# Column sums for a normalizer, tile positions of small products and whole-tile transposes in a two-layer streaming encoder

## What is computed

```
# mLSTM, per head (8 heads of 512), block by block
s = einsum('bhtd,bhsd->bhts', q, k) * d                      # pairs, "P" in the kernel
num = einsum('bhts,bhse->bhte', s, v) + a * (q @ C)
den = sum(s, axis=-1) + a * (q @ n)                          # the normalizer
h = num / maximum(abs(den), exp(-m_t))
h = head_layernorm(h) ; y = ((h + skip * xc) * silu(z)) @ w_out
# attention: keys are normed per head, then for the 32 new tokens
k = rmsnorm(kvf[..., :2048].reshape(.., 16, 128), k_norm_g)
s = einsum('bqhd,bkhd->bhqk', q, k) * 128**-0.5 + f_q - f_k  # 512 cached keys, 48 of this call
p = softmax(where(k_pos <= q_pos, s, -inf)) ; o = p @ v
```

## Time and profile before

| | us |
|---|---|
| median of three runs | 1749.39 (1748.85 to 1750.18) |
| the profiled execution | 1749.33 |
| its span, first to last instruction | 1747.3 |
| PE busy | 1722.6 (99%) |
| PE weight loads busy | 1646.8 (94%) |
| DVE busy | 1101.1 (63%) |
| ACT busy | 829.0 (47%) |
| POOL busy | 295.5 (17%) |
| mean granted TensorE clock | 0.997 of full |

### The profile page before, as it was taken

One profiled execution on the slowest core, in us unless ns is written; L12 is line 12 of the kernel. 1 busy time (PEld: TensorE's weight loads), 2 busy tenths in 40 slices (PEclk: granted clock), 3 DMA queues, 4 the chain that ended last, 5 costly groups with the idle time before them and its releaser, 6 DMA issues.

```text
span 1747.3 us, 29706 instructions
## 1 busy us (share of the span) xinstructions
PE 1722.6 (99%) x11935; PEld 1646.8 (94%) x11935; DVE 1101.1 (63%) x2075; ACT 829.0 (47%) x1375; POOL 295.5 (17%) x573
## 2 busy tenths in 40 slices
PE   7999999999999999999999999999999999999998
PEld 6999999999988999989999889999999998999998
DVE  5866666766666767667576678665435545553654
ACT  4556445554653534525345245554443545435443
POOL 1201110111222331223213212021112000000000
PEclk9999999999999999999999999999999999999999
DMA  6546554555575665756557555366558554554533
GB/s 175 171 136 207 163 183 143 181 183 173 180 222 166 195 230 162 230 166 207 198 171 242 155 167 183 118 207 204 165 195 286 160 161 139 162 175 151 156 101 111
DMA packets 244232, 309.27 MB, mean 177 GB/s; under 512 B 14008, under 2 KB 219600, under 8 KB 244096
## 3 DMA queue, kind: packets, MB, share of 16 engines
q1 hardware_dynamic: 214352, 215.32, 40.4%
q0 software_dynamic: 29200, 91.23, 15.3%
q10 hardware_dynamic: 544, 0.82, 0.2%
HBM read 260.53 MB, written 46.79 MB: 176 GB/s over the span
## 4 chain that ended last, share of the span: by engine, by line
PE 93%; DVE 2%; ACT 2%; DMA 1%; issue 1%; SPq 0%; ACTq 0%; DVEq 0%
PE acc L177 25%; PE acc L178 24%; PE acc L179 24%; PE aux L1414 4%; PE aux L1437 3%; PE aux L1298 2%; PE aux L1303 1%; PE aux L1455 1%; PE aux L1418 1%; DMA raw<-in_a_w_in 1%; PE aux L2679 1%; PE aux L1279 1%; DVE w_lo L157 1%; PE aux L1277 1%; PE aux L2668 1%; PE aux L2722 1%
## 5 line engine op out<-in xcount | busy, mean ns | idle before, releaser
L157 DVE TENSOR_TENSOR w_lo<-raw,w_hi 128x1024 fp32r<-128x1024 f32 x400 | 486.3, 1221 | 339.0 <-ACT w_hi L152 337.0
L177 PE MATMUL acc<-xg_hi,w_hi 128*128 128x304 f32 x1536 | 474.0, 309 | 2.5 <-DVE w_lo L157 2.5
L152 ACT ACTIVATE w_hi<-raw 128x1024 fp32r<-128x1024 f32 x400 | 414.3, 1054 | 122.1 <-PE acc L179 92.1
L179 PE MATMUL acc<-xg_hi,w_lo 128*128 128x304 f32 x1536 | 465.0, 303 | 0.0
L178 PE MATMUL acc<-xg_lo,w_hi 128*128 128x304 f32 x1536 | 464.4, 302 | 0.0
L177 PEld LDWEIGHTS acc<-xg_hi,w_hi 128*128 128x128 f32 x1536 | 290.6, 189 | 5.8 <-issue 2.0
L178 PEld LDWEIGHTS acc<-xg_lo,w_hi 128*128 128x128 f32 x1536 | 291.6, 190 | 0.9
L179 PEld LDWEIGHTS acc<-xg_hi,w_lo 128*128 128x128 f32 x1536 | 291.0, 189 | 0.0
L104 POOL TENSOR_TENSOR cell<-cell 1x1 f32<-1x1 f32 x159 | 70.4, 443 | 1173.9 <-DVE xc_lo L897 306.2
L177 PE MATMUL acc<-xb_hi,w_hi 128*128 128x288 f32 x512 | 156.3, 305 | 0.9 <-DVE w_lo L157 0.9
L177 PE MATMUL acc<-hz_hi,w_hi 128*128 128x304 f32 x512 | 155.3, 303 | 0.4 <-DVE zs L981 0.4
(11 more groups left out here) (537 smaller groups left out, 3220.9 us busy)
## 6 DMA issues: line engine op xcount, KB each, us to landing
raw<-in_a_w_in SPq DMA_DIRECT2D x128, 512.0 KB, 4.0
raw<-in_a_w_out SPq DMA_DIRECT2D x64, 512.0 KB, 4.4
raw<-in_w_kvf SPq DMA_DIRECT2D x64, 512.0 KB, 4.8
raw<-in_b_w_in SPq DMA_DIRECT2D x64, 512.0 KB, 4.6
raw<-in_b_w_out SPq DMA_DIRECT2D x32, 512.0 KB, 3.5
raw<-in_a_wq SPq DMA_DIRECT2D x16, 512.0 KB, 4.1
raw<-in_a_wk SPq DMA_DIRECT2D x16, 512.0 KB, 3.7
raw<-in_a_wv SPq DMA_DIRECT2D x16, 512.0 KB, 4.2
```

The lines of the kernel that those rows point to most:

```text
L152: act.activation(w_hi[:, s, :, :], raw[:, s, :, :], ACT.Copy).then_inc(hi_made, 1)
L157: dve.tensor_tensor(w_lo[:, s, :, :], raw[:, s, :, :], w_hi[:, s, :, :].bitcast(F32), ALU.subtract).then_inc(lo_made, 1)
L177: pe.matmul(acc[b][:, 0:width], wh, x_hi[:, k0 + k, :], start=st, stop=False)
L179: mm = pe.matmul(acc[b][:, 0:width], wl, x_hi[:, k0 + k, :], start=False, stop=last and k == 3)
```

## The change

It has four parts.

1. *Sums.* The products of line 1418 go, with `one` and `one_strip`. A new event D, `sums`, stands behind Z (one or three chunks before the outputs; in the first head in the same list as O): VectorE adds the second key tile's columns and the two strips of `Dm` into its first 304 columns, multiplies `aq` by `n0` for the four row tiles, adding up in `aq_sum` (a new tile of 48 columns), and adds that to the last 48 columns. PE then makes, behind all other products of `outputs` and a wait on `den_in`, three products with a 128 x 128 piece of `Dm` as weights and two columns of `ones`. They are f32.
2. *Turns of `hn`.* The third token tile, 48 rows, is transposed as 128 rows, of which VectorE clears those from 32 on once, before the first head's `norm`.
3. *Turns of `k_t`.* The same; the results stand 128 columns apart in the bank, and the copy out of it takes 48 of each.
4. *New queries.* `scores_new` takes both banks at once and makes first the eight head products, each with 32 columns of weights at a tile position (0, 32x) and the 32 output rows of its head; then the `F2` products and the mask over all rows.

```diff
-        BESIDE_OUT = {1: "E", 2: "P", 3: "Q", 4: "Z", 5: "V", 7: "O K"}
+        BESIDE_OUT = {1: "E", 2: "P", 3: "Q", 4: "Z D", 5: "V", 7: "O K"}
-        FIRST_NEXT = {0: "E", 1: "P V Q", 2: "O K Z", 3: "N", 5: "T0 T1", 6: "T2 T3 S0 S1 H0 H1",
+        FIRST_NEXT = {0: "E", 1: "P V Q", 2: "O D K Z", 3: "N", 5: "T0 T1", 6: "T2 T3 S0 S1 H0 H1",
-        END_OUT = {0: "E", 1: "P", 2: "Q", 3: "V Z", 4: "O K", 6: "T0 T1",
+        END_OUT = {0: "E", 1: "P", 2: "Q", 3: "V Z D", 4: "O K", 6: "T0 T1",
...
+            def sums(h):
+                wait(dve, p_lo_made, h + 1)
+                own.wait()
+                tail = Dm[:, 256:T]
+                own.done(dve.tensor_tensor(Dm[:, P:T], Dm[:, P:T], Dm[:, T:SP0], ALU.add))
+                own.done(dve.tensor_scalar(aq_sum[:, :], aq_head[:, 0, :], n0[:, 0:1], None, ALU.mult))
+                own.wait()
+                for d in range(1, HT):
+                    own.done(dve.scalar_tensor_tensor(aq_sum[:, :], aq_head[:, d, :], n0[:, d:d + 1], aq_sum[:, :],
+                                                      ALU.mult, ALU.add))
+                    if d < 3:
+                        c = (SP0, SS0)[d - 1]
+                        own.done(dve.tensor_tensor(Dm[0:32, 256:T], Dm[0:32, 256:T], Dm[0:32, c:c + TAIL], ALU.add))
+                    own.wait()
+                dve.tensor_tensor(tail, tail, aq_sum[:, :], ALU.add).then_inc(den_in, 1)
...
+                if (h.a, h.b) == (0, 0):
+                    own.done(dve.memset(hn[32:64, 2, :], 0.0))
+                    own.done(dve.memset(hn[64:P, 2, :], 0.0))
...
-                    sums = [(p_, one_) for p_, _, one_ in parts if one_ is not None]
-                    for k, (p_, one_) in enumerate(sums):
-                        mm = pe.matmul(aux[3][:, 2 * t:2 * t + one_.shape[-1]], p_, one_, start=k == 0,
-                                       stop=k == len(sums) - 1, skip_group_check=True)
+                wait(pe, den_in, h + 1)
+                for t in range(3):
+                    mm = pe.matmul(aux[3][:, 2 * t:2 * t + 2], Dm[:, t * P:t * P + P], ones[:, 0:2], start=True, stop=True)
...
-                    mm = pe.transpose(aux[b][:, t0:t0 + n], hn[0:n, t, m * P:(m + 1) * P], ident[0:n, 0:n])
+                    mm = pe.transpose(aux[b][:, t0:t0 + P], hn[:, t, m * P:(m + 1) * P], ident[:, :])
...
-                        mm = pe.transpose(aux[b][:, m * n:(m + 1) * n], k_t[0:n, t, m * P:(m + 1) * P],
-                                          ident[0:n, 0:n])
+                        mm = pe.transpose(aux[b][:, m * P:(m + 1) * P], k_t[:, t, m * P:(m + 1) * P], ident[:, :])
...
+                old, new = free_bank(u), free_bank(u + 1)
+                for bank, keys in ((old, KcT[:, :, :]), (new, kT_in[:, :, 256:T])):
+                    for x in range(GRP):
+                        r = x * DEC
+                        pe.matmul(bank[r:r + DEC, 0:keys.shape[-1]], q_new2[:, x * BW:x * BW + DEC], keys[:, x, :],
+                                  start=True, stop=False, tile_position=(0, r))
+                pe.matmul(old[:, 0:PAST], of_all, F2[:, FC:FC + PAST], start=False, stop=True).then_inc(use_ready, 1)
+                pe.matmul(new[:, 0:WZ], of_all, F2[:, FN:FN + WZ], start=False, stop=False)
+                pe.matmul(new[:, 0:WZ], ident_bf[:, :], tri_new[:, :], start=False, stop=True).then_inc(use_ready, 1)
```

More of the change, by code:

```diff
@@ L244, in trunk @@
         both = sb("both", [P, 3, P], F32R, ph)
-        one = sb("one", [P, 2], F32R, ph)
-        one_strip = sb("one_strip", [STRIP, 2], F32R, ph)
+        pad20 = sb("pad20", [P, 16], F32, ph)
         st = sb("st", [P, 12, 3], F32, ph)
@@ L339, in trunk @@
          v_hi_made, vt_hi_made, v_lo_made, k_hi_made, kt_hi_made, k_lo_made, den_ready,
-         den_taken, n_ready, n_taken, var_ready, root_made, gated, hz_hi_made, hz_ready,
+         den_taken, den_in, n_ready, n_taken, var_ready, root_made, gated, hz_hi_made, hz_ready,
          head_set, pads_set) = (sem("m_" + n) for n in (
@@ L343, in trunk @@
              "v_hi_made", "vt_hi_made", "v_lo_made", "k_hi_made", "kt_hi_made", "k_lo_made",
-             "den_ready", "den_taken", "n_ready", "n_taken", "var_ready", "root_made",
+             "den_ready", "den_taken", "den_in", "n_ready", "n_taken", "var_ready", "root_made",
              "gated", "hz_hi_made", "hz_ready", "head_set", "pads_set"))
@@ L987, in set_head @@
                 dve.memset(n_in[:, :], 0.0).then_inc(head_set, 1)
-                dve.memset(one[:, :].bitcast(F32), 1.0).then_inc(head_set, 1)
-                dve.memset(one_strip[0:64, :].bitcast(F32), 1.0).then_inc(head_set, 1)
-                dve.memset(one_strip[64:STRIP, :].bitcast(F32), 0.0).then_inc(head_set, 1)
                 dve.memset(both[:, :, :].bitcast(F32), 0.0).then_inc(head_set, 1)
-                dve.wait_ge(head_set, 7)
+                dve.wait_ge(head_set, 4)
                 dve.memset(both[:, 0, 0:64].bitcast(F32), 1.0).then_inc(head_set, 1)
@@ L1105, in exponents @@
                                   ALU.add).then_inc(exp_in, 1)
-                dve.tensor_tensor(aq_head[:, :, 16:TAIL], q_new[:, h.value, :, :],
-                                  a_row[:, h.value, :].unsqueeze(1).to_broadcast([P, HT, DEC]), ALU.mult)
+                own.done(dve.tensor_tensor(aq_head[:, :, 16:TAIL], q_new[:, h.value, :, :],
+                                           a_row[:, h.value, :].unsqueeze(1).to_broadcast([P, HT, DEC]), ALU.mult))
                 own.done(dve.tensor_copy(n0[:, :], par[:, bass.ds((h.times(HT) + N00).value, HT)]))
@@ L1217, in event @@
                     low_pairs(h)
+                elif e == "D":
+                    sums(h)
                 elif e == "V" and (h.a or h.b):
@@ L1405, in outputs @@
                         c = t * P if s == 0 else T + (t - 1) * P
-                        parts += [(P_hi[:, c:c + P], v_hi[:, s, :], one[:, :]),
-                                  (P_lo[:, c:c + P], v_hi[:, s, :], one[:, :]),
-                                  (P_hi[:, c:c + P], v_in[:, s, :], None)]
+                        parts += [(P_hi[:, c:c + P], v_hi[:, s, :]), (P_lo[:, c:c + P], v_hi[:, s, :]),
+                                  (P_hi[:, c:c + P], v_in[:, s, :])]
                     if t > 1:
[L1410 to L1413, removed]
+                        parts += [(P_hi[0:STRIP, c:c + P], vt[:, s, :]) for s, c in enumerate((SP0, SS0))]
+                        parts += [(aq[:, d * TAIL:d * TAIL + P], C_in[:, d, :]) for d in range(HT)]
+                    for k, (p_, v_) in enumerate(parts):
                         mm = pe.matmul(aux[b][:, :], p_, v_, start=k == 0, stop=k == len(parts) - 1)
                     mm.then_inc(b_ready, 1)
-                    sums = [(p_, one_) for p_, _, one_ in parts if one_ is not None]
-                    for k, (p_, one_) in enumerate(sums):
-                        mm = pe.matmul(aux[3][:, 2 * t:2 * t + one_.shape[-1]], p_, one_, start=k == 0,
-                                       stop=k == len(sums) - 1, skip_group_check=True)
+                wait(pe, den_in, h + 1)
+                for t in range(3):
+                    mm = pe.matmul(aux[3][:, 2 * t:2 * t + 2], Dm[:, t * P:t * P + P], ones[:, 0:2], start=True, stop=True)
                 mm.then_inc(den_ready, 1)
@@ L2058, in settings @@
                 own.done(dve.memset(ssum[:, :], 0.0))
+                own.done(dve.memset(k_t[32:64, 2, :], 0.0))
+                own.done(dve.memset(k_t[64:P, 2, :], 0.0))
                 own.wait()
```

11 lines of the change are left out of this document (6 added, 5 removed).

## The result

The changed kernel takes **1718.1 us** (median of four runs, 1716.86 to 1719.45) against 1749.12 of the kernel before (four runs beside them): a ratio of 0.982 with a 95% interval of 0.981 to 0.984, 31.0 us less. The prediction said 1722.1 with a range of 1714.5 to 1731.0. The time lies inside the range, and the sums and the turns of `hn` came close to their sizes; the keys' turns lost by their clears what they gained, and the quarters gave twice what they were put down for.

What follows compares the result with a forecast made beforehand. The prediction took PE's stream of matrix instructions as the bound (busy 1722.6 of 1747.3 us). Savings of 12.5 + 8.1 + 0.5 + 6.1 = 27.2 us took 1749.3 to 1722.1 us, range 1714.5 to 1731.

Steps and rivals of the forecast that it cites:

- Step 1: Outputs of a head: 20 normalizer-sum instructions on PE become six, saving 1.57 us a head, 12.5 us in eight heads.
- Step 2: Turns of `hn`: last tiles transposed whole, saving 0.51 us a pair, 8.1 us in 16 pairs.
- its note on the last pair: Last head's turns: the last pair may give nothing if VectorE can't follow, taking 0.5 us off at most.
- Step 3: Turns of `k_t`: last tiles transposed whole, saving 0.13 us in each of four groups, 0.5 us in all.
- Step 4: New queries' scores: head products in quarter tiles, saving 1.53 us a group, 6.1 us in four groups.
- Rival (b): New queries' products: all four quarters run at once, saving 12.5 us there; 1715.7 us in all; chance 0.20.
- Both bounds: New queries' saving a group: 0.25 us with steps one after the other, 3.12 us with all quarters at once.
- the five lengths: New queries, old keys: four quarter products take five instruction lengths, 2.15 us, giving 2.80 us a group in all.
- (a): New queries' products: quarters run one after the other, saving 1.0 us there; 1727.2 us in all; chance 0.20.
- (c): New queries' products: a drain of 0.25 us at each of seven changes of quarter; 1734.2 us; chance 0.07.
- (e): New queries' products: quarter instructions run without a pipeline, 10.2 us a group instead of 4.33; 1751.6 us; chance 0.03.
- (d): VectorE becomes late behind event D, from 3.05 us for D; 1734.4 us were D 4.8; chance 0.08.

Runs made afterwards that it cites:

- after: The changed kernel with all four parts, traced against the kernel before: 1718.1 us against 1749.12, ratio 0.982.
- only_sums: The kernel before with the normalizer sums on VectorE alone: 1736.79 us, ratio 0.992 to the kernel before.
- the halves: Two runs of the changed kernel with head products in two halves of the array instead of four quarters, in two orders: 1722.39 and 1721.94 us.
- one_quarter: The changed kernel with all four heads' products sent to the first quarter of the array, one after the other: 1729.36 us.
- slow_sums: The changed kernel with 16 more small clears behind the sums on VectorE: 1754.11 us.
- halves_grouped: The changed kernel with 64-column weights, heads 0 and 1 to one half of the array, then 2 and 3 to the other: 1722.39 us.

## Why the prediction was right, and where its sizes were off

**Step 1** held: 1.55 us a head for 1.57. The two-column products cost 0.11 each, as in the earlier trace rows, but for the first, behind which the second starts after 0.03: six in 668.87 - 668.29 = 0.58. In all 11.3 came for 12.5, since in the trace of after the first head's block has 6.8 us at half clock for 3.4 before; in only_sums, where it has 3.4, 12.7 came. The working had not taken in the clock. VectorE's cover held with 1.7 us to spare.

**Step 2** held in each pair, 0.51, and its note on the last pair was half of it: that pair gives nothing and swallows the one before as well, 7.1 for 8.1. **Step 3** was 0.13 a group, as worked out, but its clears, which "would cost 0.6 at most" where "VectorE is not waited for", cost 0.8 on PE's path: VectorE is waited for there, and the step by itself is a loss of some 0.3 us.

**Step 4** is the term that was mis-sized: 12.2 us for 6.1. The failed step is "the instructions are issued in order, so that the first of a product can run beside the second of the one before, and no more". In its place stands what the halves show: no part of the array waits for another, and four products in four quarters take two lengths. Rival (b), all at once, saved 3.12 a group by its sum and 3.05 in the trace. Both bounds were right, each now seen in a run (0.24 in one_quarter for 0.25, 3.05 for 3.12); the value between them was chosen from a rule that no row had shown, and the chances of 0.42 to 0.20 leaned the wrong way. The range held because it reached as far as (b): that 1718.1 lies in it says nothing for the five lengths, and it is nearer to (b), 1715.7, than to the forecast, 1722.1. (b) with the two shortfalls, 1715.7 + 1.2 + 1.0 = 1717.9, comes near 1718.1, in part by luck, since the 1.2 is the half clock of one trace.

**Rivals** (a), (c) and (e) are refuted by the starts 7 ns apart. (d) was right in kind, as slow_sums shows, but begins at 3.6 us of D, not 3.05, and D takes 1.87. The chances for its price were made without the clock: behind a wait of 3.4 us it can cost nearly half as much again.

## What to carry to other kernels

Where several small products have their own rows of the result, give them as few columns of weights as those rows and a column position each: they run beside each other, and the whole costs what the fullest position costs. Where a tile is narrower than its neighbours, compare the change of tile (0.25 us here for 48 rows) with the columns it saves. Before work is moved to another engine, look for the room in front of the one that is waited for, for a single clear too (two of them cost 0.8 us here), and count a wait of TensorE of some microseconds with the stretch at half clock that may come behind it.

## What was not expected of the hardware

An instruction for a free half of the array starts beside the first of the other half though it is the fifth in order (halves_grouped, four lengths of 0.43 instead of six or more; the pairing is inferred, as said above). Two instructions of one f32 product in the same quarter are 0.43 apart, those of other quarters 0.007. And a wait of PE can cost more than itself: the granted clock fell to half for 3.4 or 6.8 us at the end of waits of 2.7 to 5.3 us, except one of 3.4, and not behind those of 0.8; but it fell too behind one of 0.65 with twelve one-column products after it, in two of the eight traces that have it.
